# A gated residual behind a dense layer: the running sum goes into x during the last down unit, and the last products are read from PSUM

## What is computed

```python
def run_layer(l, x, c, buf, pos, chunk):
    sh1, sc1, gt1, sh2, sc2, gt2 = adaln_params(c, ada_w[l], ada_b[l])
    h = modulate(x, norm1_g[l], sh1, sc1)
    z = h @ w_in[l]
    ...
    x = x + gt1 * mix
    h = modulate(x, norm2_g[l], sh2, sc2)
    if l % 2 == 0:
        f = swiglu(h, ffn_w1[l // 2], ffn_w3[l // 2], ffn_w2[l // 2])
    else:
        f = moe_swiglu(h, router_w[l // 2], moe_w1[l // 2], moe_w3[l // 2], moe_w2[l // 2])
    x = x + gt2 * f
```

## Time and profile before

| | us |
|---|---|
| median of 3 runs | 1606.2 |
| lowest and highest run | 1604.25, 1611.41 |
| span of the profiled execution | 1602.8 |

### The profile page before, as it was taken

The page is one execution under the profiler, slowest core; times in us unless marked ns, Lnnn a source line. Parts: engine busy times, 40 slices in busy tenths (PEclk is TensorE's granted clock), DMA queues, the critical chain, the costliest instruction groups (busy, mean ns, idle before and its releaser), DMA issues.

```text
span 1602.8 us, 22201 instructions
## 1 busy us (share of the span) xinstructions
PE 1561.0 (97%) x8225; PEld 1324.7 (83%) x8225; DVE 1185.8 (74%) x972; ACT 954.2 (60%) x738; POOL 75.1 (5%) x115
## 2 busy tenths in 40 slices
PE   7899999999999997999999999999999999999997
PEld 4678799999996787888888888888888888888885
DVE  3564544444455556888888888888888898889997
ACT  3353433333334433778778777777777777777774
POOL 4200000000001001000000000000000000001001
PEclk9998999999999986999999999999999999999999
DMA  9876864444438673999999999999999999999993
GB/s 346 315 270 240 305 230 137 156 146 142 157 115 314 215 246 111 357 369 362 405 377 369 396 375 364 402 374 368 399 376 367 399 377 370 395 370 373 396 383 136
DMA packets 249771, 493.01 MB, mean 308 GB/s; under 512 B 10091, under 2 KB 16107, under 8 KB 249722
## 3 DMA queue, kind: packets, MB, share of 16 engines
q1 hardware_dynamic: 241318, 472.82, 80.7%
q0 software_dynamic: 6112, 19.10, 3.3%
q10 hardware_dynamic: 2308, 0.64, 0.2%
HBM read 482.39 MB, written 10.36 MB: 307 GB/s over the span
## 4 chain that ended last, share of the span: by engine, by line
PE 92%; DMA 3%; DVE 3%; issue 1%; ACT 1%; POOL 1%; SPq 0%; ACTq 0%; DVEq 0%
PE ps L1669 19%; PE ps L1671 19%; PE ps L1670 19%; PE ps L1947 4%; PE ps L1949 4%; PE ps L1948 4%; PE ps L1688 2%; PE ps L1959 2%; PE ps L1957 2%; PE ps L1958 2%; PE ps L2103 1%; DMA raw<-in_ada_w 1%; PE ps L1903 1%; PE ps L1905 1%; PE ps L1904 1%; PE ps L1831 1%
## 5 line engine op out<-in xcount | busy, mean ns | idle before, releaser
L1072 DVE TENSOR_TENSOR w_lo<-raw,w_hi 128x2048 fp32r<-128x2048 f32 x366 | 835.7, 2291 | 177.9 <-ACT w_hi L711 176.6
L711 ACT ACTIVATE w_hi<-raw 128x2048 fp32r<-128x2048 f32 x366 | 701.9, 1918 | 264.3 <-PE ps L1671 163.0
L1669 PE MATMUL ps<-w_hi,split 128*128 128x512 f32 x1392 | 549.7, 395 | 1.0 <-DVE sp_ L1114 0.9
L1671 PE MATMUL ps<-w_hi,split 128*128 128x512 f32 x1392 | 543.5, 390 | 0.0
L1670 PE MATMUL ps<-w_lo,split 128*128 128x512 f32 x1392 | 542.8, 390 | 0.0
L1669 PEld LDWEIGHTS ps<-w_hi,split 128*128 128x128 f32 x1392 | 262.1, 188 | 57.2 <-DVE w_lo L1072 3.3
L1671 PEld LDWEIGHTS ps<-w_hi,split 128*128 128x128 f32 x1392 | 261.8, 188 | 55.7
L1670 PEld LDWEIGHTS ps<-w_lo,split 128*128 128x128 f32 x1392 | 262.3, 188 | 52.5
L1947 PE MATMUL ps<-split,w_hi 128*128 128x320 f32 x448 | 138.6, 309 | 0.0
L1948 PE MATMUL ps<-split,w_hi 128*128 128x320 f32 x448 | 138.4, 309 | 0.0
L1949 PE MATMUL ps<-split,w_lo 128*128 128x320 f32 x448 | 138.4, 309 | 0.0
(11 more groups left out here) (341 smaller groups left out, 1375.2 us busy)
## 6 DMA issues: line engine op xcount, KB each, us to landing
raw<-in_moe_w SPq DMA_DIRECT2D x336, 1024.0 KB, 7.3
raw<-in_ada_w SPq DMA_DIRECT2D x48, 1024.0 KB, 7.7
raw<-in_ffn_w SPq DMA_DIRECT2D x42, 1024.0 KB, 5.0
raw<-in_w_in SPq DMA_DIRECT2D x12, 1024.0 KB, 9.5
raw<-in_w_out SPq DMA_DIRECT2D x8, 1024.0 KB, 9.3
item_rows<-plain POOLq DMA_DIRECT2D x12, 512.0 KB, 7.6
plain<-in_x_prompt SPq DMA_DIRECT2D x2, 512.0 KB, 3.9
split<-mod_rows SPq DMA_DIRECT2D x2, 512.0 KB
```

What stands on the lines that cost most here:

```text
L711: a.activation(w_hi[:, (s0 + j) % SPL], raw[:, (u0 + j) % RAW], ACT.Copy).then_inc(hi_ready, 1)
L1072: v.tensor_tensor(w_lo[:, (s0 + j) % SPL], raw[:, (u0 + j) % RAW], w_hi[:, (s0 + j) % SPL].bitcast(F32), ALU.subtract).then_inc(lo_ready, 1)
L1669: t_.matmul(out, a_hi, b_hi, start=first_, stop=False)
L1671: return t_.matmul(out, a_lo, b_hi, start=False, stop=last_)
```

## The change

On VectorE, the addition of unit 40 to the sum is left out. As soon as units 38 and 39 are in the sum, `residual_part` adds gate times sum to all four pairs of x, without signalling. The last products (unit 40 for the lower pairs, unit 41 for the upper) are then added by `residual` directly from PSUM, and the two additions of the upper pairs to the sum fall away. The low part of I0 moves from between the two lower and the two upper pairs to behind the last pair. The low part of I1 moves from ahead of the norm into it, behind the low part of the second pair of h. No other engine's program is changed.

```diff
@@ -1198,6 +1198,7 @@
             if n < 3:
                 lo_pair(1)
             if n == 2:
+                lo_to(S_IN[1] + 2)
                 ada_add(*PRE_MOD[1])
             scale_pair(3)
             if n < 3:
@@ -1312,6 +1313,17 @@
 
         pairs = [0]
 
+        def residual_part(l, mod_chunk, k, src):
+
+            gt = mod[:, l, mod_chunk + k:mod_chunk + k + 2, :]
+            for q in range(2):
+                v.scalar_tensor_tensor(out=x[:, k + q, 0:NP_TOK], in0=src[:, q, 0:NP_TOK], scalar=gt[:, q, 0:1],
+                                       in1=x[:, k + q, 0:NP_TOK], op0=ALU.mult, op1=ALU.add)
+            step(v.tensor_tensor(smp[:].rearrange("p k (b t) -> p k b t", t=TS),
+                                 src[:, :, NP_TOK:T].rearrange("p k (b t) -> p k b t", t=TS),
+                                 gt[:, :, 1:ROWS].unsqueeze(3).to_broadcast([P, 2, NSEQ, TS]), ALU.mult))
+            step(v.tensor_tensor(x[:, k:k + 2, NP_TOK:T], x[:, k:k + 2, NP_TOK:T], smp[:], ALU.add))
+
         def residual(l, mod_chunk, k, src):
 
             gt = mod[:, l, mod_chunk + k:mod_chunk + k + 2, :]
@@ -1396,24 +1408,19 @@
         ffn_add(0, s1 + 35, 12)
         lo_to(cur[0] + 1)
         ffn_add(1, s1 + 36, 13)
-        ffn_add(0, s1 + 37, 14)
-        ve.wait_ge(f_add, 15)
+        ve.wait_ge(f_add, 14)
+        for k in range(0, KD, 2):
+            residual_part(0, 5 * KD, k, facc[:, k:k + 2, :])
+        ve.wait_ge(split_used, s1 + 37)
         for k in range(0, KB, 2):
-            residual(0, 5 * KD, k, facc[:, k:k + 2, :])
-        lo_to(S_IN[1] + 1)
-        ve.wait_ge(f_add, 15)
+            residual(0, 5 * KD, k, ps[:, k:k + 2, :])
         for k in range(KB, KD, 2):
             if k == KB:
                 ve.wait_ge(half_down, 1)
             else:
                 ve.wait_ge(split_used, s1 + 38)
-            half = facc[:, k:k + 2, :]
-            v.tensor_tensor(half, half, ps[:, k:k + 2, 0:T], ALU.add).then_inc(f_add, 1)
-            ve.wait_ge(f_add, 16 + (k - KB) // 2)
-            residual(0, 5 * KD, k, half)
-
-
-        lo_to(S_IN[1] + 2)
+            residual(0, 5 * KD, k, ps[:, k:k + 2, :])
+        lo_to(S_IN[1] + 1)
         norm(1, 0)
         project_in(1)
         mixer(1)
```

## The result

The changed kernel takes 1617.23 us (median of 5 runs, 1615.66 to 1619.25), the kernel before 1604.25 us in the same comparison (5 runs, 1603.52 to 1611.41). The ratio is 1.0080 with a 95% interval of 1.0062 to 1.0098: 13.0 us slower, and by the interval between 10 and 16 us. The forecast was 1619.7 us in a range of 1614.0 to 1624.5, by +13.5 us.

The account below looks back on a forecast made before the run. The prediction took TensorE as the bound (92% of the chain), with its wait for a weight load deciding. 10.8 + 2.7 = +13.5 us on a 1602.8 us span gave 1616.3, plus 3.4 around it 1619.7 us; range 1614.0 to 1624.5.

Parts of the forecast that it names:

- step 1: VectorE after unit 39: four early gate updates hide beside units 40 and 41, releasing unit 40 0.2 us late; uncovered 5.7 us.
- step 2: VectorE's last updates: reading PSUM takes 0.88 us as from SBUF, three additions go, x is complete 2.35 us sooner.
- step 3: Behind the dense layer: TensorE's sixteen square-sum matmuls take 4.57 us and become the limit, so 1.6 us is gained, not 2.35.
- step 4: I0's low part behind the last update: P2's first load is issued at 482.3 instead of 478.03, alone costing nothing.
- step 5: I1's low part in the norm: P2's second load is issued 12.9 us later, TensorE waits, the input projection starts 10.8 us later.
- step 6: After the wait TensorE restarts at 1.2 GHz: 0.8 us in half a block, 1.9 in dense matmuls, +2.7 us together.
- step 7: Loads queued behind P2's second load: I2's low part is done at 520.7, TensorE arrives at 524.4 or later; 3.7 us spare.
- Nothing behind takes the delay in: Stages after I2: work keeps its distances, and no wait for anything outside the chain could absorb a delay.
- the gain arrives and P2b is not late: Rival: the norm's input ends sooner and P2's second load does not hang on I1's low part; -1.6 us, 1604.6, chance 0.07.
- The stall without the clock: Rival: TensorE waits for P2's second load but keeps 2.4 GHz; +10.8 us, 1617.0, chance 0.08.
- The loads behind P2b cost time too: Rival: loads issued right behind P2's second load share the engines, so it lands 2.8 us later; 1622.5, chance 0.07.
- The sum of +13.5 us: Whole kernel: 10.8 us later projection start, with the 1.6 us gain already in it, plus 2.7 us for the clock.

Follow-up runs that it names:

- e2: Changed kernel with both low parts (I0's, I1's) at their old places, leaving only early gate updates and reading from PSUM; ratio 0.9994.
- e1: Changed kernel with I1's low part back ahead of the norm, behind I0's low part; ratio 1.0000.
- e3: Kernel before with only I1's low part moved into the norm, behind the low part of the second pair of h; ratio 1.0091.
- e5: Changed kernel with I1's low part one pair earlier in the norm, behind the low part of the first pair of h; ratio 1.0053.
- e4: Changed kernel with modulation block P2 placed inside I0 on TensorE, ahead of its last quarter, instead of ahead of I0; ratio 1.0063.
- e6: Changed kernel with 22 extra fp32 matmuls on TensorE between the two halves of block P2, where it otherwise waits; ratio 1.0047.
- e8: On top of e2, ScalarE makes the high part of each pair of h right behind its own shift in this norm; 1602.82 us, ratio 0.9975.

## Why the prediction was right, and where it was off

- **The early gate updates cost nothing** (step 1): right. They end at 470.4; unit 40 is done 471.54 - 464.50 = 7.04 us behind unit 39 in the kernel before, which is 470.18 here, so the delay is 0.2 to 0.3 us (0.2 forecast).
- **Reading from PSUM costs nothing** (step 2): right, 0.88 us for the two large instructions in both places.
- **The gain is 1.6 us, not 2.35, since TensorE's square sums become the bound** (step 3): right. e2 shows the block of sixteen in one piece and a distance to I0 shorter by 14.54 - 12.89 = 1.65 us.
- **I0's low part costs nothing where it was moved** (step 4): right for the changed kernel, where P2a's half of the block runs at 485.98 without a wait. It is not free in general: e1 differs from e2 by this move alone and is 1.9 us worse in the distance to I0, 0.9 us of it by the clock. In the changed kernel P2b is issued 15.1 us behind P2a (495.98 - 480.85), in e1 2.2 us.
- **P2b's issue hangs on I1's low part, and TensorE stands behind it** (step 5): right, and this is shown from both sides: e3 has the loss with this line alone, e1 has none without it, and e5 moves the line by 4.0 us and the wait by 3.9. The wait was forecast at 14.2 us (488.5 to 502.7) and measured at 13.97.
- **The clock** (step 6): the mechanism was right, the size stands at the upper part of what is seen: 2.7 us forecast, 1.4 us in the first profile, 2.6 us in the second (0.9 in P2 and 1.7 behind). The mis-sized term is the dense stretch at the lower rate, 1.9 us forecast and 0.5 to 1.9 measured in five profiles. The step also misread a row: the 2 us in the routing stage are the width of a window of the earlier trace rows; TensorE's idle time that ends at 627.96 there is 4.99 us. A wait of 14 us is longer than that too, but e1 has the clock fall after 2.7 us.
- **The loads behind P2b have room** (step 7): right, 6.0 us where 3.7 were counted, for I2 came 17.9 us behind P2b's issue, not 19.0, and TensorE reached it 28.1 us behind that issue (524.10 - 495.98), not 26.9. e4 shows how near the second limit is.
- **Nothing behind takes the delay in**: right, by the last columns of the table.
- **The rivals**: "the gain arrives and P2b is not late" fell with the row of the queue at 495.98. "The stall without the clock" fell with the windows at 0.50 and with e6. "The loads behind P2b cost time too" fell in the form that was given: P2b with its company behind it was used 5.0 to 5.3 us after its issue in the kernel before, the changed one (twice), e3, e4, e5 and e6, in all of which TensorE waited for it (in the kernel before only its weight loading, 0.60 us, and the block was no longer for it: 1.92 us). The one case that took longer is e1, with 6.9 us and the same company behind; there another load stood 2.2 us *ahead*. That this is the cause rests on one run.

The sum of +13.5 us came out as +13.0 us by the medians, and as +11.8 us from the square sum to I2 in the first profile, +13.3 us in the second. The wait and the gain make 11.3 to 11.6 us of it up to I0, half a block at the lower clock included; without it that is 10.4 to 10.7 us, where the sum had 10.8. The agreement of the medians to 0.5 us is closer than the clock's term allows, and in part luck.

The median itself came out 2.5 us under the forecast of 1619.7, for the most part by the base: the kernel before has its median at 1604.25 us with five runs, where the forecast took 1606.2 from three. The 3.4 us "around" the span were mis-sized as well. A run of the kernel before takes 2.0 us more than its span (1605.23 against 1603.2 us in one), a run of the changed kernel 1.7 (1615.66 against 1614.0); the other 1.4 us were the distance of one profiled execution from the median.

## What to carry to other kernels

Where loads are issued in one order into a ring of buffers, a conversion that looks idle (its unit is needed only much later) is also the credit for the load a ring length further on, so before it is moved, name that load and who stands in line for it. A late load also shifts every load queued behind it; taking its own consumer out of the way only exposes the next arrival. And when a gap has been shortened, look for which short idle time ends last now: here the order of two ScalarE instructions was worth 1.3 us, the whole gate part 1.65.

## What was not expected of the hardware

- Two 1 MB loads 2.2 us apart in one queue, in one run (e1): the second is used 6.9 us after its issue, against 5.0 to 5.3 us for one that finds the queue empty, with or without further loads issued 0.4 to 1 us behind it.
- The granted clock came back after 1.1 us of dense matmuls (502.88 to about 504) in one profile of the changed kernel and after nearly 4 us (502.58 to about 506.5) in another, with waits of 14.0 and 14.3 us and the same half block of 1.94 us ahead.
- A wait of 2.69 us in e1 was followed by the lower clock (0.50 in the window 492 to 494), the waits of 2.0 us ahead of I0 in the kernel before and in e2 were not: I0 to I2 took 20.7 us there, at the full rate.
- The first 478 us, the same program up to the last two down units, scatter by 5 us between profiles (476.4 to 481.7), more than the whole gain of e8. Differences of 1 to 2 us can be seen only from a common point in the trace.
